# Conditioning in half-K chunks turned by transpositions, means subtracted on GpSimd, and a token-major final norm in a two-layer fp32 decoder trunk

## The reference

```
c_act = silu(c)
for l in range(2):
    mod = c_act @ w_ada[l] + b_ada[l]                 # [9, 6*1024]
    sh1, sc1, gt1, sh2, sc2, gt2 = split(mod, 6)
    h = x * (1 + sc1) + sh1
    y = token_mixer(h, ...)                           # input projection, gMLP + HGRN2, output projection
    x = layer_norm(ALPHA * x + gt1 * y, ln1_w, ln1_b)
    h = x * (1 + sc2) + sh2
    y = swiglu(h) if l == 0 else moe_swiglu(h)        # 8 experts, top 2
    x = layer_norm(ALPHA * x + gt2 * y, ln2_w, ln2_b)
```

## Time and profile before

| | |
|---|---|
| median of 3 runs | 1637.14 us (1635.72 to 1642.07) |
| profiled execution | 1640.02 us, span 1638.3 us |
| mean granted TensorE clock | 0.968 |
| busy share of the span: PE, DVE, ACT, POOL | 94%, 72%, 57%, 2% |
| DMA | 415.08 MB, mean 253 GB/s |

### The profile page before, as it was taken

How to read it: one execution, slowest core, us unless ns; L and a number is a source line. 1 busy time by engine, 2 the same in 40 slices (tenths; PEclk the granted TensorE clock), 3 DMA queues, 4 the chain that set the end, 5 groups by cost and what they waited for, 6 DMA issues and landing times.

```text
span 1638.3 us, 23457 instructions
## 1 busy us (share of the span) xinstructions
PE 1543.7 (94%) x9130; PEld 1315.0 (80%) x9130; DVE 1171.9 (72%) x1232; ACT 925.8 (57%) x897; POOL 39.7 (2%) x76
## 2 busy tenths in 40 slices
PE   6899998799999799988899999999999999999995
PEld 3777877699999699876678788888887888888883
DVE  2433457755556855665788988889898898988985
ACT  2443526343333465462776767676676776767763
POOL 2000010000000010000000000000000000000000
PEclk9899989999999899989999999999999999999998
DMA  9999954254444253132499999999999999999991
GB/s 314 323 349 292 334 149 136 77 180 146 143 149 154 78 150 127 49 110 65 152 349 354 350 312 360 342 362 353 317 360 336 364 345 319 359 346 368 342 362 57
DMA packets 242034, 415.08 MB, mean 253 GB/s; under 512 B 7891, under 2 KB 128893, under 8 KB 241926
## 3 DMA queue, kind: packets, MB, share of 16 engines
q1 hardware_dynamic: 238662, 402.31, 71.6%
q0 software_dynamic: 3264, 11.28, 2.4%
HBM read 406.75 MB, written 6.82 MB: 252 GB/s over the span
## 4 chain that ended last, share of the span: by engine, by line
PE 47%; DVE 4%; DMA 3%; ACT 3%; issue 1%; POOLq 0%; ACTq 0%; DVEq 0%
PE bank L620 13%; PE bank L622 13%; PE bank L621 13%; DVE w_lo L1550 1%; DMA raw_ring<-in_e_up_dram 1%; DMA raw_ring<-in_e_gate_dram 1%; ACT w_hi L1267 1%; PE bank L1056 1%; PE bank L1018 1%; PE bank L724 1%; PE bank L623 1%; PE bank L625 1%; PE bank L624 1%; PE bank L739 1%; PE bank L1101 1%
## 5 line engine op out<-in xcount | busy, mean ns | idle before, releaser
L1550 DVE TENSOR_TENSOR w_lo<-raw_ring,w_hi 128x2048 fp32r<-128x2048 f32 x264 | 604.4, 2291 | 103.4 <-ACT w_hi L1267 102.4
L1267 ACT ACTIVATE w_hi<-raw_ring 128x2048 fp32r<-128x2048 f32 x264 | 506.6, 1919 | 230.4 <-PE bank L622 208.1
L620 PE MATMUL bank<-w_hi,xg_hi 128*128 128x512 f32 (+1 forms) x768 | 293.2, 382 | 1.9 <-DVE xg_lo L2048 1.7
L622 PE MATMUL bank<-w_hi,xg_lo 128*128 128x512 f32 (+1 forms) x768 | 288.7, 376 | 0.0
L621 PE MATMUL bank<-w_lo,xg_hi 128*128 128x512 f32 (+1 forms) x768 | 288.2, 375 | 0.0
L623 PE MATMUL bank<-act_hi,w_hi 128*128 128x320 f32 x736 | 236.6, 322 | 27.0 <-DVE act_lo L1600 20.3
L624 PE MATMUL bank<-act_lo,w_hi 128*128 128x320 f32 x736 | 231.8, 315 | 0.0
L625 PE MATMUL bank<-act_hi,w_lo 128*128 128x320 f32 x736 | 231.7, 315 | 0.0
L1541 DVE TENSOR_TENSOR w_lo<-raw_ring,w_hi 128x2048 fp32r<-128x2048 f32 x65 | 148.6, 2287 | 100.9 <-ACT w_hi L1199 100.7
L623 PEld LDWEIGHTS bank<-act_hi,w_hi 128*128 128x128 f32 x736 | 142.8, 194 | 36.3 <-issue 30.6
L622 PEld LDWEIGHTS bank<-w_hi,xg_lo 128*128 128x128 f32 x768 | 144.2, 188 | 29.3
(11 more groups left out here) (318 smaller groups left out, 1980.5 us busy)
## 6 DMA issues: line engine op xcount, KB each, us to landing
raw_ring<-in_e_gate_dram SPq DMA_DIRECT2D x90, 1024.0 KB, 5.4
raw_ring<-in_e_up_dram SPq DMA_DIRECT2D x90, 1024.0 KB, 5.3
raw_ring<-in_e_down_dram SPq DMA_DIRECT2D x88, 1024.0 KB, 5.2
raw_ring<-in_w_ada_dram SPq DMA_DIRECT2D x24, 1024.0 KB, 7.7
raw_ring<-in_w_in_dram SPq DMA_DIRECT2D x24, 1024.0 KB, 7.7
st<-in_w_ada_dram SPq DMA_DIRECT2D x12, 1024.0 KB, 8.6
kdsp<-in_w_ada_dram SPq DMA_DIRECT2D x12, 1024.0 KB, 10.0
raw_ring<-in_w_ff_gate_dram SPq DMA_DIRECT2D x11, 1024.0 KB, 5.3
```

The costliest lines, as they stand in the source:

```text
L620: pe.matmul(out, xh, wh, start=start, stop=False)
L622: return pe.matmul(out, xl, wh, start=False, stop=stop)
L1267: act.activation(w_hi[:, (NSPLIT + i) % SPL, :], raw[:, s, :], ACT.Copy).then_inc(hi_ready.sem, 1)
L1550: dve.tensor_tensor(w_lo[:, r, :], raw[:, s, :], w_hi[:, r, :].bitcast(F32), ALU.subtract).then_inc(lo_ready.sem, 1)
```

## The change

1. **Conditioning.** A chunk is half of K by 512 columns: 4 matmuls of 512 columns, DRAM rows of 2 KB instead of 1 KB. Two chunks are a pair p. ScalarE copies 128x512 once per pair into `wide`. TensorE turns the pair by four transpositions into the pair's own bank; VectorE sums the four partial sums by a `tensor_reduce` into bank 0 (`ada_sums`), at one place in each window (`ada_turned`). The first matmul of pair p waits for the sum of the last pair in its bank.
2. **Means.** Quarters 1 to 3 of `minus_mean` are on GpSimd, in three of the norms; VectorE's `normalise` waits for `less_mean`.
3. **MoE start.** GpSimd scales `xT`, ScalarE no longer; `accT` is not cleared, expert 0's `scattered` copies into it; the constant `before` is made late.
4. **Gather.** Two fills stand in each of experts 0 to 5 (blocks 3 and 4), instead of four in each of experts 1, 3 and 5.
5. **Tail.** What `accT` holds after seven experts goes into `xT` during expert 7 (`flush_prompt`, `flush_samples`); expert 7's results go straight into `xT` with the gate (`add_gated`); TensorE transposes x per m; the norm is token-major on VectorE from PSUM, with rows of ln2's weight and bias that GpSimd loads during expert 7.

```diff
@@ conditioning, TensorE
-                for kk in range(KD):
-                    g = kk % 4
-                    last = pe.matmul(b[32 * g:32 * g + 32, 0:CW], cT[:, kk, :], w[:, kk, :],
-                                     start=(kk < 4), stop=(kk >= KD - 4))
+                for g in range(4):
+                    last = pe.matmul(b[32 * g:32 * g + 32, :], cT[:, 4 * half + g, :], w[:, g, :],
+                                     start=(half == 0), stop=(half == 1))
                 last.then_inc(ada_used.sem, 1)
-                if i - adas[0] == 1:
+                if half == 0 and p - adas[0] == 1:
                     ada_turn()
             def ada_turn():
-                if l and c == 0:
-                    pe.wait_ge(mod_read.sem, mod_read.at(0, 1))
-                if l == 0 and c == ADA_A:
-                    pe.wait_ge(mod_read.sem, mod_read.at(0, 0))
-                pe.wait_ge(ada_row.sem, i + 1)
-                for m in range(2):
-                    o = (2 * c + m) * NC
-                    last = pe.matmul(bank[0][:, o:o + NC], nmean[:, m * P:(m + 1) * P], pick[:], start=True, stop=True)
+                pe.wait_ge(ada_row.sem, p + 1)
+                for m in range(4):
+                    last = pe.transpose(bank[ada_bank(p)][:, m * P:(m + 1) * P], wide[:, m * P:(m + 1) * P], ident[:])
@@ conditioning, VectorE
+            def ada_sums(p):
+                c = p % (NADA // 2)
+                dve.wait_ge(ada_T.sem, p + 1)
+                dve.tensor_reduce(bank[0][:, 4 * NC * c:4 * NC * (c + 1)].rearrange("p (m c) -> p m c", c=NC),
+                                  bank[ada_bank(p)][:, :].rearrange("p (m g c) -> p m c g", m=4, g=4)[:, :, 0:NC, :],
+                                  AX.X, ALU.add).then_inc(ada_sum.sem, 1)
@@ means, GpSimd
+            def minus_mean(l, i):
+                pool.wait_ge(md_ready.sem, md_ready.at(l, i))
...
+                pool.wait_ge(sum_mm.sem, sum_mm.at(l, i))
+                for a in range(1, 4):
+                    ks = slice(2 * a, 2 * a + 2)
+                    pool.tensor_tensor(xT[:, ks, :], xT[:, ks, :], lnx[:, 3, :].unsqueeze(1).to_broadcast([P, 2, T]),
+                                       ALU.subtract).then_inc(less_mean.sem, 1)
@@ MoE start, GpSimd
-            pool.memset(accT[:], 0.0).then_inc(sc_read.sem, 1)
+            for kk in range(KD):
+                last = pool.tensor_scalar(xT[:, kk, :], xT[:, kk, :], lnA[:, DEPTH - 1, kk:kk + 1],
+                                          lnA[:, DEPTH - 1, KD + kk:KD + kk + 1], ALU.mult, ALU.add)
@@ gather, all engines
-                        if b in (3, 4) and odd:
-                            fill(rd, (e + 1) // 2, 3 * (b - 3))
+                        if b in (3, 4) and more:
+                            fill(rd, e // 2 + 1, 2 * (e % 2) + b - 3)
@@ tail, TensorE
             for m in range(KD):
-                sums(DEPTH - 1, 1, m)
...
+                pe.wait_ge(x_added.sem, rounds * KD + (m + 1))
+                for t in range(2 if m in (4, 5) else NT):
+                    turn_out(m, t)
@@ tail, VectorE
+                if e == NE - 1:
+                    add_gated(m, b, 5 * KD, (sc_read.sem, sc_read.at(rd, KD * e + m)), (sc_read.sem, 1)).then_inc(x_added.sem, 1)
...
-            add_channels(DEPTH - 1)
-            deviation(DEPTH - 1, 1)
-            for a in range(4):
-                normalise(DEPTH - 1, 1, a)
+            for half, t in H2:
...
+                last = dve.bn_stats(fstat[0:n, t, half, :], bank[OUT_BANK[NT * half + t]][0:n, :])
...
+                last = dve.bn_aggr(fmv[0:n, t, 0:2], fstat[0:n, t, :, :])
...
+                dve.scalar_tensor_tensor(xtok[0:n, t, cols], bank[OUT_BANK[i]][0:n, :], fmv[0:n, t, 0:1], ln_rows[0:n, 0, cols],
+                                         ALU.subtract, ALU.mult).then_inc(f_scaled.sem, 1)
...
+                dve.scalar_tensor_tensor(xtok[0:n, t, cols], xtok[0:n, t, cols], fmv[0:n, t, 3:4], ln_rows[0:n, 1, cols],
+                                         ALU.mult, ALU.add).then_inc(out_done[i].sem, 1)
```

More of the change, by code:

```diff
@@ L48, in hybrid_trunk @@
     NT = len(TILES)
+    VTILES = [(0, 0, P), (1, P, P), (2, TP, TS)]
+    H2 = [(half, t) for half in range(2) for t in range(NT)]
+    OUT_BANK = (0, 1, 2, 4, 6, 5)
+    POOL_OUT = (0, 1)
     CW = 256
@@ L370, in hybrid_trunk @@
         sc_read = signal("sc_read", NE * KD, base=1)
+        flushed = signal("flushed", 2)
+        x_added = signal("x_added", KD, base=KD)
+        fin_in = signal("fin_in")
         out_T = signal("out_T", 2)
[L372 removed]
+        f_var = signal("f_var")
+        f_sd = signal("f_sd")
+        f_scaled = signal("f_scaled")
+        f_rs = signal("f_rs")
+        f_by_rs = signal("f_by_rs")
+        out_done = [signal(f"out_done{i}") for i in range(2 * NT)]
         outs = signal("outs")
@@ L485, in _ @@
                                     pattern=[[-1, P]], channel_multiplier=1))
-            link(pool.memset(cT[:], 0.0))
-            link(pool.memset(pick[:], 0.0))
-            for g in range(4):
-                ins = pool.affine_select(out=pick[:], in_=pick[:], compare_op=ALU.not_equal, fill=1.0, base=-32 * g,
-                                         pattern=[[-1, NC]], channel_multiplier=1)
-                if g < 3:
-                    link(ins)
-            ins.then_inc(consts.sem, 1)
+            pool.memset(cT[:], 0.0).then_inc(consts.sem, 1)
             pool.wait_ge(consts.sem, 1)
             link(pool.memset(ones[:], 1.0))
-            link(pool.affine_select(out=before[:], in_=ones[:], compare_op=ALU.is_ge, fill=0.0, base=-1,
-                                    pattern=[[1, P]], channel_multiplier=-1))
             link(pool.memset(lvl_mask[:], 0.0))
@@ L604, in hybrid_trunk @@
         TOP_K = 2
-        H2 = [(half, t) for half in range(2) for t in range(NT)]
         MW = P + 2 * NE
         NROWS = 7 * DEPTH + 1
-        VTILES = [(0, 0, P), (1, P, P), (2, TP, TS)]
         def sum_banks(i):
@@ L1110, in experts @@
                 for e in range(NE):
-                    odd = e % 2 and e < NE - 1
+                    more = e < NE - 2
                     gate_up(rd, e, "gate", 0, 0)
@@ L1139, in experts @@
                             scatter(rd, e - 1, 6 * (b - 1) + 1)
-                        if b == 3 and odd:
-                            fill(rd, (e + 1) // 2, 1)
                         if parts[b] == 2:
@@ L1151, in experts @@
                                 scatter(rd, e - 1, 3)
-                            if b == 3 and odd:
-                                fill(rd, (e + 1) // 2, 2)
                             down(rd, e, b - 1, 1)
@@ L1477, in experts @@
                             turned(rd, e, 0)
-                        if b in (3, 4) and odd:
-                            gathered(rd, (e + 1) // 2, 3 * (b - 3))
+                        if b in (3, 4) and more:
+                            gathered(rd, e // 2 + 1, 2 * (e % 2) + b - 3)
                         if parts[b] == 2:
@@ L1483, in experts @@
                         used(rd, e, "up", b, 0)
-                        if b == 3 and odd:
-                            gathered(rd, (e + 1) // 2, 1)
                         if parts[b] == 2:
@@ L1647, in modulation, with add_gated @@
                 dve.wait_ge(mod_read.sem, mod_read.at(l, part))
-            def gated(m, b, gt, ready, read):
+            def add_gated(m, b, gt, ready, read):
                 dve.scalar_tensor_tensor(xT[:, m, 0:TP], b[:, 0:TP], modT[:, gt + m, 0:1], xT[:, m, 0:TP], ALU.mult, ALU.add)
@@ L1927, in gather_down @@
                             dve.wait_ge(d_added.sem, d_added.at(c - 1, m))
-                            last = gated(m, bank[5 + i % 3], 5 * KD, (d_read.sem, d_read.at(c - NFC + 2, m)), (d_read.sem, 1))
+                            last = add_gated(m, bank[5 + i % 3], 5 * KD, (d_read.sem, d_read.at(c - NFC + 2, m)), (d_read.sem, 1))
                             if c < NFC - 1:
@@ L2128, in experts @@
                         used(rd, e, "up", b, 0)
-                        if b == 3 and odd:
-                            gathered(rd, (e + 1) // 2, 1)
+                        if e == NE - 1 and b in (3, 4):
+                            flush_prompt(rd, range(4 * (b - 3), 4 * (b - 2)))
                         if e == 0 and b in (1, 2):
```

224 lines of the change are left out of this document (142 added, 82 removed).

## The result

The changed kernel takes 1614.88 us (median of 4 runs, 1611.51 to 1617.73) against 1638.36 of the kernel before (4 runs): ratio 0.9854, 95% interval 0.9825 to 0.9883. Timed once more beside the last experiments it was 1615.95 against 1638.57, ratio 0.9855 (0.9831 to 0.9879). Forecast were 1604.0 with a range of 1594 to 1616: the side and the range hold, the range by 1.1 us only, and the narrower 1598 to 1610 of the forecast's own mechanism does not. Of the 33 us forecast 23 came.

The account below looks back on a forecast made before the run. TensorE, busy 94% of the span, was taken as the bound. Terms -14.3 (conditioning), -1.6, -2.9, -1.5, +0.5, -13.3 sum to -33.1 from 1640.0; less 2.9 to the median, 1604.0 us, range 1594 to 1616 (own mechanism 1598 to 1610, chance 0.62).

Parts of the forecast that it names:

- Head: Before the first modulation: 2 KB rows land chunks faster and one turn less stands in the way, -1.3 us.
- Turns: Conditioning in the windows: one turn of four transpositions per pair of chunks replaces a turn per chunk, -11.4 us.
- Pauses: Conditioning: TensorE's two pauses from the old turn, at 91.68 and 125.42, and the slow clock after go, -4.6 us.
- new waits: Conditioning: TensorE waits for VectorE's sums, +2.0, and for chunks wanted sooner from busy DMA, +1.0; together +3.0 us.
- The first rival: Windows: TensorE waits about 1 us for sums in most of 9 windows, clock falling after; total 1613, chance 0.15.
- Norms: GpSimd's subtractions take one VectorE instruction off the path in two norms, -0.8 each, -1.6 us; third norm 0.
- hidden: Norms: GpSimd's three subtractions, 4.9 us, end before VectorE's next subtraction and so cost nothing.
- the shared port: Norms, tail, MoE start: GpSimd and VectorE hinder each other; norms +2.5, total 1610 us, chance 0.09.
- MoE start: Before the first fill: TensorE no longer waits for GpSimd's memset of the accumulator, -2.9 us.
- Gather: Expert 0: fills moved there are partly free while ScalarE waits for weights from DMA, -1.5 us.
- Flush: Last expert: VectorE's 8 flushes and two more, 5.3 us in all, delay TensorE's low parts, +0.5 us.
- Tail: After the last expert: additions, statistics and final norm on VectorE form a shorter chain, -13.3 us.

Follow-up runs that it names:

- sums_early: Changed kernel with window 3's first partial sum before VectorE's low part and scan, and one sum of windows 8 and 9 before the differences; windows 165.56 us, span 1606.1.
- rows_late: Changed kernel with the two 512 KB row loads issued after the last weight chunk has been read; windows 167.56 us, span 1612.5.
- combined: Changed kernel with early sums, means split between GpSimd and VectorE, late scalings, spread flush and a third output tile on ScalarE and GpSimd; 1605.87 us, ratio 0.9801.
- the middle: Middle of the windows stage over the kernels that leave the sums at their late place (167.56 to 171.65 us): 170.2 us.
- norm_dve: Changed kernel with all subtractions of the mean back on VectorE; norm 8.06 us, third norm 5.45, span 1613.9.
- gather_old: Changed kernel with the four fills of each gather in experts 1, 3 and 5 again; experts 0 to 6 716.44 us, span 1614.2.

## Why the prediction was right or wrong, point by point

- **Head, -1.3**: measured -1.25. That they agree is partly luck, since two sizes beneath were wrong and nearly cancel: a chunk takes 2.71 us, not 2.87, which makes the landing 2.2 sooner instead of 1.0, and the last sum waited about 1 us behind VectorE's low parts, a wait that I had not counted.
- **Turns, -11.4**: off in size. I took a group of four transpositions at the 0.44 of the earlier trace rows; in the stream they take 0.58 before a chunk and 0.41 before a product, 10.9 us for twenty instead of 8.8. The old ones, by the same reading (start of a turn to start of what follows), took 19.85 for the 39 in the windows instead of 20.2 for forty. That makes -8.9.
- **Pauses, -4.6, and new waits, +3.0**: the old pauses went. The new ones were priced right in sum, 2.48 + 0.57 = 3.05 against 2.0 and 1.0, but put in the wrong window and without the clock, which fell after 94 as it had after 125: about 1.7 us by its 0.83. "About 1 us of slack" in window 3 was read against TensorE's old pace; with its turns cheaper TensorE came 1.0 us too soon. The other 1.47 of that pause is ScalarE's wait for a weight chunk, which is what I had put at +1.0 for DMA; it came through VectorE's order and not as a wait of TensorE for weights. Early sums are worth 2.0 us where the chunk is on time in both (sums_early beside rows_late) and 3.9 where it is not (`combined` beside the middle). The first rival had such waits in most of nine windows; they came in two.
- **Norms, -1.6**: wrong, +1.8 in three norms. The step that failed is "hidden": GpSimd's three instructions were sized right (5.10 against 4.9), but VectorE's two on the path were slowed. I had the shared port as a rival at 0.09 and priced it at +2.5 for the norms. Its mechanism is what happened, at less than its price: GpSimd's instructions take 1.53 to 2.11, not the 3 of the rival. The third norm, which I left at 0, lost 1.16, and norm_dve gives it back (5.45).
- **MoE start, -2.9**: the memset's wait is gone, but the router beside GpSimd's scalings got 0.55 us longer (6.82 against 6.27), by VectorE's slowed comparisons, and the fills 0.7 longer (8.88 against 8.15) at a mean clock of 0.69 instead of 0.80. -1.3.
- **Gather, -1.5**: wrong. gather_old shows it. What I moved was sized right (2.36 us for two fills against 2.4, though "two such per fill" would have made it 4.8), but nothing hid it: ScalarE's waits for DMA were not TensorE's.
- **Flush, +0.5**: mis-sized, 1.5, since four stood in one piece ahead of a low part. Expert 7's 2.8 us more than before have the late down chunk in them too.
- **Tail, -13.3**: measured -14.2, nearly term by term: 6.4 forecast and 6.6 measured for the eight additions, 3.7 and 3.7 for the statistics.

The total stayed inside the range because the range had been drawn to take in the rivals, not because the terms held: windows, norms, MoE start and experts together came 12 us short of their forecast, and only the tail gave 0.9 more.

## What to carry to other kernels

Work moved to GpSimd is free only under VectorE instructions that do not want its ports: before moving it, list what VectorE runs in those microseconds, and put the pieces under the reciprocal, reductions and subtractions that read PSUM, which kept their times here (`tensor_scalar` did not). A gate that hangs on one place in another engine's order is to be checked against the new pace of the waiting engine, not the old. It hands on every late landing ahead of it, and its price is the pause and, in half of the runs here, a slow clock behind it. An idle stretch of the engine itself, such as the 3.95 us before the last low part, is where small work goes.

## What the runs showed of the hardware that I had not expected

- VectorE beside GpSimd: subtraction and multiplication of 640 columns from SBUF 1.34 to 1.47 us instead of 0.82, `tensor_scalar` of 128 columns 0.35 instead of 0.21; reciprocal (2.15) and PSUM-with-SBUF instructions (1.27 for two of 512 columns) unchanged. The slowed one ends 0.68 after GpSimd's instruction has ended.
- The windows of the same code differ by up to 4 us between executions (167.6 to 171.7). The shortest has the shortest pause in window 3 (0.98) and a full clock behind it, the longest the longest pause (3.21) and a clock of 0.66 for 5 us.
- A 1 MB load with 2 KB rows lands 2.71 us after the one before it (387 GB/s), with 1 KB rows 3.00 (349), with all DMA engines busy in both.
